# A two-layer decoder trunk: the norm's factor moved from y to the gate sums and the down outputs, y-combinations formed one stage earlier, two plain pairs per layer instead of six

## The chip, the core and the metric

One of the eight cores of a Trainium2 chip runs the whole program. The metric is device time in microseconds (us) of one execution, the lower the better.

## What is computed

The input is one sequence of 512 tokens with 1024 features, in float32. Layer 0 mixes tokens with an mLSTM and a differential attention, layer 1 with a sparse attention (compressed, selected and window branches). Behind each mixer stands a gated feed-forward block, and at the end a norm. The change touches the feed-forward block, the output projection ahead of it and the residual sums behind it:

```python
def rmsnorm(x, g):
    y = xf * lax.rsqrt(jnp.mean(xf * xf, axis=-1, keepdims=True) + RMS_EPS)
    return y * g
...
def swiglu_ffn(h, norm_g, w_gate, w_up, w_down):
    y = rmsnorm(h, norm_g)
    return (jax.nn.silu(y @ w_gate) * (y @ w_up)) @ w_down
...
    h = h + mixer(...) @ w_out
    h = h + swiglu_ffn(h, ...)
```

FFN_HIDDEN is 2816, so w_gate and w_up have 22 blocks of 128 columns each. The factor of the norm is one number per token; below it is called the norm's factor (rinv in the code). The gain g is one number per feature.

## The kernel before

**Layout.** Everything is kept feature-major: 128 partitions hold 128 features, and the free dimension is the 512 tokens (T), so a 1024-feature array is eight blocks of 128x512 (KT = 8). Each float32 operand of a product is split in two: a high part (a copy to the type fp32r, made by ScalarE) and a low part (the rest, made by VectorE), and a product is three matmuls: high by high, high by low, low by high. w_high and w_low are the split weights, y_high and y_low the split input.

**The stream of weights.** The weights come in units of 128 output columns (UNIT_LIST), through a ring of four raw buffers that SyncE fills and two pairs of split buffers. A plain unit is eight feature blocks by three matmuls, 24 matmuls of 128x512. All engines run their own hand-written list in order and wait for each other by semaphores.

**The stages around the change**, once per layer: WO (8 units, output projection; VectorE adds each unit's result to the residual hT, ScalarE makes y_high with the gain, VectorE y_low, ScalarE the square, GpSimd adds the squares up in sum_square), UP (gate and up products), DN (down projection, 16 half units, residual add in down_post). TensorE turns the sum of squares into columns (norm_columns, L993), GpSimd takes the power -1/2, VectorE spreads it (norm_diag) and TensorE lays the factor out over the partitions (norm_rows, L998) into bank aux 1; ScalarE copies it to rinv. norm_columns stands behind the first UP unit in TensorE's list and norm_rows behind the second.

**Plain pairs.** A pair is block t of w_gate and block t of w_up. The first PLAIN = 6 pairs of a layer are two plain units each. Their y has the gain and not the norm's factor; VectorE multiplies the factor in when it takes a result out of its bank (take, L2173), ScalarE applies silu, GpSimd multiplies gate and up (L3054), ScalarE and VectorE split the product into ffn_high and ffn_low.

**Fast pairs.** The other NFAST = 16 pairs use a product of 2x2 blocks with seven block products instead of eight. Weights are combined into the forms A11, A12, S2, S1, S3, S4, A22 and the input into B11, B21, T2, T1, T3, B22, T4; a block product is 4 by 3 matmuls of 128x256, 84 matmuls for a pair. fast_quad is TensorE's list: the seven products in this order, with waits for the forms (form_low) and, before S2, S3, S4 and A22, for ScalarE to have copied the bank's half (part_taken, fast_copy, L1887), because three products are added up in the same half bank and intermediate sums are taken on the way. Since the input forms are made from scaled y, VectorE first makes eight blocks y_scaled (L2497, with gain and factor), then the sums T1, T2, T3, T4 (y_sum, 128x1024 each) and the seven low parts, all during the plain pairs.

For each fast pair VectorE's list in fast_up is, for pair t in the middle of the stage: s24_low and s13_low of t (L2572, L2566), fast_take of t-1 (L2586), first_sums of t+1 (L2550), the two halves of fast_product of t-1 (L2594, L2596), a22_low of t (L2578), gate_form_low of t+1 (L2539), ffn_low of t-1 (L2481), second_sums of t+1 (L2559, L2561). ScalarE's: a22_high, fast_copy A11, fast_silu of t-1 (L1893), gate_form_high of t+1 (L1844), fast_copy S2, fast_ffn_high of t-1, fast_copy S1, fast_copy S3, s24_high and s13_high of t+1 (L1862, L1853). GpSimd adds one 128x256 pair of partial sums (up_late, L3059), released by fast_copy S3.

The lines that say how a fast pair's gate sum gets to silu, on VectorE and ScalarE, are

```python
dve.wait_ge(S("part_taken"), 4 * fast_quads(layer, t) + 2)
dve.tensor_tensor(a, ps(tile)[:, :], a, ALU.add).then_inc(bank_free(tile), 1)
...
wait_taken(act, (f"UP{layer}", 2 * t))
act.activation(a, a, ACT.Silu).then_inc(S("silu"), 1)
```

## Time and profile before

| | before |
|---|---|
| median of 3 runs | 1299.47 us (1298.99 to 1299.5) |
| profiled execution, its own time | 1298.77 us |
| its span | 1297.0 us |
| TensorE matmul busy, share | 1285.3 us, 99% |
| TensorE weight loads busy, share | 1084.0 us, 84% |
| VectorE | 868.4 us, 67% |
| ScalarE | 654.4 us, 50% |
| GpSimd | 203.9 us, 16% |
| granted TensorE clock | full in all 40 slices |
| HBM | 95 GB/s over the span |

The span runs from the first to the last instruction of the profiled execution, and the execution's own time stands 1.77 us above it. Matmuls are pipelined and overlap in the records, so that the start of one to the start of the next is the pace of TensorE, not the duration of one. Likewise a VectorE or ScalarE instruction that waits for nothing starts a little before the one ahead of it has ended. In the timeline's rows the text in brackets is the idle time ahead of the instruction and what ended it.

### The profile page before, as it was taken

What the parts mean: (1) busy time and instruction counts of PE and PEld (TensorE: products, weight loads), DVE (VectorE), ACT (ScalarE), POOL (GpSimd) and SP (SyncE); (2) the same over time, 40 slices, a digit from 0 to 9 for tenths busy, and PEclk for the clock granted to TensorE, in tenths of its full rate; (3) what the DMA queues carried; (4) which work ended last, traced back from release to release, by engine and by line L of the source; (5) the groups of instructions that cost most, each with busy time, mean ns of one, the idle gap of its engine ahead of it and who ended that gap; (6) DMA issues with size and microseconds to landing.
All of it is one profiled execution on the core that took longest, in us unless ns stands there. A gap on an engine that the chain in (4) does not pass through costs nothing.

```text
span 1297.0 us, 20009 instructions
## 1 busy us (share of the span) xinstructions
PE 1285.3 (99%) x7568; PEld 1084.0 (84%) x7568; DVE 868.4 (67%) x1522; ACT 654.4 (50%) x1214; POOL 203.9 (16%) x212
## 2 busy tenths in 40 slices
PE   9999999999999999999999999999999999999997
PEld 7777788888999998888788865568888999998887
DVE  5678886558888884232699778776477888872222
ACT  4445765434566563222275457785444565652222
POOL 2003571222100011000000002112213101110100
PEclk9999999999999999999999999999999999999999
DMA  8332222342433348332244310000432334455311
GB/s 257 82 82 62 56 65 72 90 147 82 113 98 99 104 120 255 94 89 81 82 123 130 95 33 17 2 2 25 140 112 81 98 99 117 112 138 165 106 44 66
DMA packets 207177, 124.40 MB, mean 96 GB/s; under 512 B 5841, under 2 KB 203729, under 8 KB 206321
## 3 DMA queue, kind: packets, MB, share of 16 engines
q1 hardware_dynamic: 205936, 113.03, 30.9%
q10 hardware_dynamic: 736, 9.84, 2.0%
q0 software_dynamic: 416, 0.35, 0.3%
q8 instruction: 56, 0.92, 0.3%
q14 instruction: 33, 0.26, 0.1%
HBM read 116.92 MB, written 6.29 MB: 95 GB/s over the span
## 4 chain that ended last, share of the span: by engine, by line
PE 88%; DVE 6%; issue 2%; ACT 2%; POOL 2%; DMA 0%; SPq 0%; POOLq 0%; DVEq 0%; ACTq 0%
PE acc L881 12%; PE acc L883 11%; PE acc L882 11%; PE acc L1201 8%; PE acc L1203 8%; PE acc L1204 8%; PE acc L1532 3%; PE acc L894 2%; PE acc L895 2%; PE acc L898 2%; PE aux L1519 2%; PE aux L1439 2%; POOL work L3054 2%; DVE w_low L730 1%; PE acc L935 1%
## 5 line engine op out<-in xcount | busy, mean ns | idle before, releaser
L730 DVE TENSOR_TENSOR w_low<-raw_units,w_high 128x1024 fp32r<-128x1024 f32 (+1 forms) x120 | 161.7, 1347 | 233.2 <-ACT w_high L711 233.1
L711 ACT ACTIVATE w_high<-raw_units 128x1024 fp32r<-128x1024 f32 (+2 forms) x121 | 136.7, 1129 | 221.3 <-PE acc L883 183.2
L881 PE MATMUL acc<-y_high,w_high 128*128 128x512 f32 (+1 forms) x360 | 144.8, 402 | 0.0
L881 PE MATMUL acc<-ffn_high,w_high 128*128 128x512 f32 (+1 forms) x374 | 141.0, 377 | 0.0
L882 PE MATMUL acc<-ffn_low,w_high 128*128 128x512 f32 (+1 forms) x374 | 140.8, 377 | 0.0
L883 PE MATMUL acc<-ffn_high,w_low 128*128 128x512 f32 (+1 forms) x374 | 140.8, 377 | 0.0
L883 PE MATMUL acc<-y_high,w_low 128*128 128x512 f32 (+1 forms) x360 | 140.7, 391 | 0.0
L882 PE MATMUL acc<-y_low,w_high 128*128 128x512 f32 (+1 forms) x360 | 140.3, 390 | 0.0
L1201 PE MATMUL acc<-high_T,s_s_forms 128*128 128x256 f32 x384 | 108.8, 283 | 2.0 <-DVE s_s_forms L2572 2.0
L1204 PE MATMUL acc<-high_T,s_s_forms 128*128 128x256 f32 x384 | 108.7, 283 | 0.0
L1203 PE MATMUL acc<-low_T,s_s_forms 128*128 128x256 f32 x384 | 108.7, 283 | 0.0
L1887 ACT ACTIVATE work<-acc 128x256 f32<-128x256 f32 x128 | 49.2, 384 | 66.6 <-PE acc L1204 64.1
L882 PEld LDWEIGHTS acc<-ffn_low,w_high 128*128 128x128 f32 x374 | 70.4, 188 | 12.9
L883 PEld LDWEIGHTS acc<-ffn_high,w_low 128*128 128x128 f32 x374 | 70.4, 188 | 12.8
L881 PEld LDWEIGHTS acc<-ffn_high,w_high 128*128 128x128 f32 x374 | 70.4, 188 | 12.7
L883 PEld LDWEIGHTS acc<-y_high,w_low 128*128 128x128 f32 (+1 forms) x360 | 67.0, 186 | 15.3
L3059 POOL TENSOR_TENSOR work<-work 128x256 f32<-128x256 f32 x32 | 34.7, 1085 | 284.9 <-ACT work L1887 284.9
L881 PEld LDWEIGHTS acc<-y_high,w_high 128*128 128x128 f32 (+1 forms) x360 | 67.2, 187 | 14.5 <-issue 0.8
L882 PEld LDWEIGHTS acc<-y_low,w_high 128*128 128x128 f32 (+1 forms) x360 | 67.2, 187 | 14.1 <-issue 0.5
L2099 ACT ACTIVATE score<-score,neg_max 128x384 f32<-128x384 f32 (+3 forms) x128 | 68.7, 541 | 18.7 <-DVE neg_max L2918 18.5
L3040 POOL TENSOR_TENSOR work<-work,work 128x512 f32<-128x512 f32 x31 | 42.1, 1357 | 225.2 <-ACT work L1625 224.8
L1201 PEld LDWEIGHTS acc<-high_T,s_s_forms 128*128 128x128 f32 x384 | 73.7, 192 | 2.3 <-DVE s_s_forms L2572 2.3
(410 smaller groups left out, 3313.7 us busy)
## 6 DMA issues: line engine op xcount, KB each, us to landing
raw_units<-in_l_w_gate_dram SPq DMA_DIRECT2D x44, 512.0 KB, 5.2
raw_units<-in_l_w_up_dram SPq DMA_DIRECT2D x44, 512.0 KB, 4.0
raw_units<-in_l_w_down_dram SPq DMA_DIRECT2D x32, 704.0 KB, 4.7
raw_units<-in_l_w_in_dram SPq DMA_DIRECT2D x43, 512.0 KB, 3.9
raw_units<-in_l_w_out_dram SPq DMA_DIRECT2D x16, 512.0 KB, 4.0
residual_spill<-residual ACTq DMA_DIRECT2D x2, 2048.0 KB, 7.4
residual<-residual_spill ACTq DMA_DIRECT2D x2, 2048.0 KB, 10.8
raw_units<-in_l_w_in_dram SPq DMA_DIRECT2D x10, 256.0 KB, 3.1
```

What stands on the lines that cost most here:

```text
L711: act.activation(dst, src, ACT.Copy).then_inc(S("split_high"), 1)
L730: dve.tensor_tensor(dst, src, high.bitcast(F32), ALU.subtract).then_inc(S("split_low"), 1)
L881: pe.matmul(o, ah, bh, start=first, stop=False)
L882: pe.matmul(o, ah, bl, start=False, stop=False)
L883: return pe.matmul(o, al, bh, start=False, stop=last)
L1201: pe.matmul(out, wh_k, y_high_of[y][:, c], start=start and k == 0, stop=False, skip_group_check=True)
L1203: pe.matmul(out, wh_k, y_low_of[y][:, c], start=False, stop=False, skip_group_check=True)
L1204: mm = pe.matmul(out, wl_k, y_high_of[y][:, c], start=False, stop=(k == KT // 2 - 1), skip_group_check=True)
L1532: mm = pe.matmul(ps(("OB", b))[64 * g:64 * g + 64, :].rearrange("p (h q) -> p h q", q=P), vsw[:, v:v + HD], probs[:, 4 * g:4 * g + 4, col(s)],
L1887: act.activation(dst, src, ACT.Copy).then_inc(S("part_taken"), 1)
L2099: act.activation(probs_at(n), probs_at(n), ACT.Exp, scale=-1.0, bias=nmx[:, n % 16:n % 16 + 1], accum_out=rsum[:, n % 16:n % 16 + 1]).then ...
L3040: pool.tensor_tensor(tmp[0][:, 0:T], tmp[0][:, 0:T], tmp[1 + m % 2][:, 0:T], ALU.add)\
```

## The change

The line numbers in the code shift by up to about 60. What it does:

- PLAIN goes from 6 to 2 in both layers, NFAST from 16 to 20; the plain path for a layer without fast pairs, which no layer used, goes away.
- The input forms are made from y with the gain and without the norm's factor. So y_scaled and its eight VectorE instructions go, and B11, B21 and B22 are no forms of their own any more: fast_quad reads quarters of y_high and y_low.
- ScalarE writes y a third time, as plain float32 (y_raw), in each WO unit. VectorE makes T1, T2, T3, T4 from it in the last four WO units (y_sums, four 128x256 instructions per unit, released by the square's semaphore sq). The high part of T2 stands on ScalarE ahead of the split of the third UP unit, T1's and T3's behind the split of the fourth; T4's goes where y's B12 quarter lies, behind the last plain unit.
- fast_take multiplies the gate sum by the factor in aux bank 1, with one more VectorE instruction that waits for the one ahead of it. The up sums stay without the factor.
- down_post multiplies the down projection's output by rinv before it is added to the residual, again one more instruction that waits for the one ahead; so do the two halves of the last tile. For it ScalarE copies the factor to rinv again at the end of UP.
- In plain pairs VectorE multiplies gate and up itself when it takes the up result (ffn_post), and GpSimd's product goes.
- Some semaphores are merged (s_recip into s_coef, rinv_count, parts_summed); loads, their sizes and their order on SyncE's queue follow the same table with more fast units.

```diff
-FAST = (0, 1)
-PLAIN = 6
+PLAIN = 2
...
-Y_FORMS = ("B11", "B21", "T1", "B22", "T2", "T3", "T4")
+Y_SUMS = ("T2", "T1", "T3", "T4")
...
@@ fast_quad, TensorE
-                    if t == PLAIN:
+                    if t == PLAIN and y in Y_SUMS:
                         pe.wait_ge(S("form_low"), y_split(layer, y))
...
@@ post of a WO unit, ScalarE
                     norm_y(n, j)
                     if j == 7:
                         split_high(act, u + SPL)
+                    act.activation(y_raw[:, tcol(j)], hT[:, tcol(j)], ACT.Copy, scale=par[:, gain_at(n, j)])
                     square(n, j)
...
@@ fast_up, ScalarE
-                hi_at = {3: ["B11"], 4: ["B21"], 5: ["T1"], 6: ["B22"], 7: ["T2"], 8: ["T3"], 9: ["T4"]}
+                hi_at = {1: ["T1", "T3"]}
                 act.dma_start(spill, hT).then_inc(S("residual_moved"), 16)
+                y_form_high(layer, "T2")
                 for c in range(2 * PLAIN):
...
                     ffn_post(layer, c // 2, c % 2)
+                y_form_high(layer, "T4")
                 for t in range(PLAIN, HT):
                     a22_high(layer, t)
                     fast_copy(layer, t, "A11")
...
                 fast_silu(layer, HT - 1)
+                act.activation(rinv, aux[:, 1, :], ACT.Copy).then_inc(S("rinv"), 1)
...
@@ post of a WO unit, VectorE
                     norm_low(1 + 2 * int(name[2]), j)
                     if j == 7:
                         split_low(dve, u + SPL)
+                    if j >= 4:
+                        y_sums(int(name[2]), j - 4)
...
+            def y_sums(layer, k):
...
+                dve.wait_ge(S("sq"), 16 * layer + k + 5)
+                dve.tensor_tensor(t1, b11, b12, ALU.subtract).then_inc(S("form_sums"), 1)
+                dve.wait_ge(S("form_sums"), base + 1)
+                dve.scalar_tensor_tensor(out=t2, in0=t1, scalar=-1.0, in1=b22, op0=ALU.mult, op1=ALU.subtract)\
+                   .then_inc(S("form_sums"), 1)
+                dve.tensor_tensor(b12, b22, b12, ALU.subtract).then_inc(S("form_sums"), 1)
+                dve.wait_ge(S("form_sums"), base + 2)
+                dve.scalar_tensor_tensor(out=t4, in0=t2, scalar=-1.0, in1=b21, op0=ALU.mult, op1=ALU.subtract)\
+                   .then_inc(S("form_sums"), 1)
...
@@ fast_take, VectorE
-                dve.tensor_tensor(a, ps(tile)[:, :], a, ALU.add).then_inc(bank_free(tile), 1)
+                dve.tensor_tensor(a, ps(tile)[:, :], a, ALU.add).then_inc(S("part_summed"), 1)
+                dve.wait_ge(S("part_summed"), parts_summed(layer, t))
+                dve.tensor_tensor(a, a, aux[:, 1, :], ALU.mult).then_inc(bank_free(tile), 1)
...
@@ down_post, VectorE
-                dve.tensor_tensor(hT[:, tile_at(m, it, 2)], ps(tile)[:, :], hT[:, tile_at(m, it, 2)], ALU.add)\
-                   .then_inc(bank_free(tile), 1)
+                h, part = hT[:, tile_at(m, it, 2)], tmp[3][:, 0:T]
+                dve.tensor_tensor(part, ps(tile)[:, :], rinv, ALU.mult).then_inc(S("part_summed"), 1)
+                dve.wait_ge(S("part_summed"), parts_summed(layer, HT - 1, m) + it * 2)
+                dve.tensor_tensor(h, part, h, ALU.add).then_inc(bank_free(tile), 1)
...
@@ fast_up, VectorE
-                scaled_at = {1: (0, 1, 2), 2: (3, 4, 5), 3: (6, 7)}
-                sum_at = {3: 1, 4: 2, 5: 3, 7: 4}
-                low_at = {4: ["B11"], 5: ["B21"], 6: ["T1", "B22"], 7: ["T2"], 8: ["T3"], 9: ["T4"]}
+                low_at = {1: ["T2", "T1", "T3"]}
...
                     if t > PLAIN:
                         fast_take(layer, t - 1)
                     else:
+                        y_form_low(layer, "T4")
                         ffn_low(layer, t - 1)
...
@@ ffn, GpSimd
-                def product(t, it=0):
...
-                    pool.tensor_tensor(up, tmp[2 * (t % 2)][:, 0:T], up, ALU.mult).then_inc(S("ffn_prod"), 1)
```

**VectorE, a fast pair in the middle of the stage.** work is the buffer of a gate or up sum, acc a PSUM bank, s_s_forms the forms S1 to S4, aux bank 1 the norm's factor. Before:

```order
L2572 TENSOR_TENSOR s_s_forms<-raw_units,s_s_forms 128x2x512
L2566 TENSOR_TENSOR s_s_forms<-s_s_sums_149,s_s_forms 128x2x512
L2586 TENSOR_TENSOR work_62<-acc,work_62 128x512
L2550 TENSOR_TENSOR s_s_sums_148<-raw_units 128x2x512
L2594 SCALAR_TENSOR_TENSOR work_63<-work_63,work_62 128x256
L2596 SCALAR_TENSOR_TENSOR work_63<-acc,work_62 128x256
L2578 TENSOR_TENSOR a_low<-raw_units,a_high 128x512
L2539 TENSOR_TENSOR gate_form_low<-raw_units,gate_form_high 128x1024
L2481 TENSOR_TENSOR ffn_low<-work_63,ffn_high 128x512
L2559 TENSOR_TENSOR raw_units<-s_s_sums_148,raw_units 128x512
L2561 TENSOR_TENSOR raw_units<-raw_units 128x512
```

and now:

```order
L2529 TENSOR_TENSOR s_s_forms<-raw_units,s_s_forms 128x2x512
L2523 TENSOR_TENSOR s_s_forms<-s_s_sums_140,s_s_forms 128x2x512
L2543 TENSOR_TENSOR work_60<-acc,work_60 128x512
L2545 TENSOR_TENSOR work_60<-work_60,aux 128x512
L2507 TENSOR_TENSOR s_s_sums_141<-raw_units 128x2x512
L2553 SCALAR_TENSOR_TENSOR work_61<-work_61,work_60 128x256
L2555 SCALAR_TENSOR_TENSOR work_61<-acc,work_60 128x256
L2535 TENSOR_TENSOR a_low<-raw_units,a_high 128x512
L2496 TENSOR_TENSOR gate_form_low<-raw_units,gate_form_high 128x1024
L2467 TENSOR_TENSOR ffn_low<-work_61,ffn_high 128x512
L2516 TENSOR_TENSOR raw_units<-s_s_sums_141,raw_units 128x512
L2518 TENSOR_TENSOR raw_units<-raw_units 128x512
```

Behind fast_take (the line with acc,work) stands the multiply by aux; all else is in the order it had.

**VectorE, the last two WO units.** y_raw is y with the gain, raw_T a raw T1, T2 or T4. Before:

```order
L2149 SCALAR_TENSOR_TENSOR y_low_164<-residual,feature_params,y_high_156 128x512
L2388 TENSOR_TENSOR residual<-acc,residual 128x512
L2149 SCALAR_TENSOR_TENSOR y_low_165<-residual,feature_params,y_high_157 128x512
L730 TENSOR_TENSOR w_low_57<-raw_units,w_high_56 128x1024
L730 TENSOR_TENSOR w_low_59<-raw_units,w_high_58 128x1024
L2162 TENSOR_SCALAR msq<-aux 128x4
```

and now:

```order
L2115 SCALAR_TENSOR_TENSOR y_low<-residual,feature_params,y_high 128x512
L2440 TENSOR_TENSOR raw_T_143<-y_raw 128x256
L2442 SCALAR_TENSOR_TENSOR raw_T_144<-raw_T_143,y_raw 128x256
L2444 TENSOR_TENSOR y_raw<-y_raw 128x256
L2446 SCALAR_TENSOR_TENSOR raw_T_145<-raw_T_144,y_raw 128x256
L2354 TENSOR_TENSOR residual<-acc,residual 128x512
L2115 SCALAR_TENSOR_TENSOR y_low<-residual,feature_params,y_high 128x512
L734 TENSOR_TENSOR w_low_57<-raw_units,w_high_56 128x1024
L2440 TENSOR_TENSOR raw_T_143<-y_raw 128x256
L2442 SCALAR_TENSOR_TENSOR raw_T_144<-raw_T_143,y_raw 128x256
L2444 TENSOR_TENSOR y_raw<-y_raw 128x256
L2446 SCALAR_TENSOR_TENSOR raw_T_145<-raw_T_144,y_raw 128x256
```

Four instructions (raw_T, raw_T, y_raw, raw_T) stand between a unit's y_low and the next unit's residual sum, and four behind the split of the second UP unit's weights, ahead of the split of the third's and of msq.

**ScalarE, the way into the first fast pair.** ffn_high is made from the product of the last plain pair, a_high is A22's high part, and the line work<-acc is the copy that TensorE's S2 waits for. Before:

```order
L1862 ACTIVATE s_s_forms<-raw_units 128x2x512
L1853 ACTIVATE s_s_forms<-s_s_sums_149 128x2x512
L1808 ACTIVATE ffn_high<-work_63 128x512
L1871 ACTIVATE a_high<-raw_units 128x512
L1887 ACTIVATE work_60<-acc 128x256
L1844 ACTIVATE gate_form_high<-raw_units 128x1024
```

and now:

```order
L1842 ACTIVATE s_s_forms<-raw_units 128x2x512
L1833 ACTIVATE s_s_forms<-s_s_sums_141 128x2x512
L1791 ACTIVATE ffn_high<-work_63 128x512
L1812 ACTIVATE y_high<-raw_T_145 128x4x256
L1851 ACTIVATE a_high<-raw_units 128x512
L1864 ACTIVATE work_60<-acc 128x256
L1824 ACTIVATE gate_form_high<-raw_units 128x1024
L1864 ACTIVATE work_60<-acc 128x256
```

The high part of T4 (y_high<-raw_T) stands between ffn_high and A22's; all else is in the order it had.

## Rows read from the trace of the kernel before

**Rows 1.** Windows view, fast pairs of layer 0: PE, PEld, DVE, ACT, POOL busy, clock, DMA.

```profile
334.40:497.00 162.60, 161.61 (x1346) 161.40 (x1346) 133.93 (x173) 98.76 (x160) 18.66 (x17) 1.00 0.40 107
```

**Rows 2.** Timeline, TensorE: last WO unit, first UP unit, norm_rows (start, us, instruction, [idle]).

```profile
261.87 0.39 PE L881 MATMUL acc<-mix_high_m,w_high 128*128 128x512 f32 x1
...
267.31 0.39 PE L881 MATMUL acc<-y_high,w_high 128*128 128x512 f32 x1
...
279.14 1.02 PE L998 MATMUL aux<-work,shape_constants 128*128 128x512 f32 x2
```

**Rows 3.** Timeline, VectorE, one fast pair in the middle of layer 0.

```profile
355.66 1.23 DVE L2572 TENSOR_TENSOR s_s_forms<-raw_units,s_s_forms 128x1024 fp32r<-128x1024 f32 x1 [1.65 <-ACT s_s_forms L1862]
...
357.94 0.68 DVE L2586 TENSOR_TENSOR work<-acc,work 128x512 f32<-128x512 f32 x1
...
359.67 0.42 DVE L2594 SCALAR_TENSOR_TENSOR work<-work,work 128x256 f32<-128x256 f32 x1
...
362.08 0.68 DVE L2481 TENSOR_TENSOR ffn_low<-work,ffn_high 128x512 fp32r<-128x512 f32 x1
362.68 0.69 DVE L2559 TENSOR_TENSOR raw_units<-s_s_sums,raw_units 128x512 f32<-128x512 f32 x1
363.40 0.69 DVE L2561 TENSOR_TENSOR raw_units<-raw_units 128x512 f32<-128x512 f32 x1
```

**Rows 4.** Timeline, ScalarE, the same pair.

```profile
357.45 0.38 ACT L1887 ACTIVATE work<-acc 128x256 f32<-128x256 f32 x1 [0.35 <-PE acc L1204]
358.66 0.63 ACT L1893 ACTIVATE work<-work 128x512 f32<-128x512 f32 x1 [0.82 <-DVE work L2586]
359.20 1.04 ACT L1844 ACTIVATE gate_form_high<-raw_units 128x1024 fp32r<-128x1024 f32 x1
360.33 0.39 ACT L1887 ACTIVATE work<-acc 128x256 f32<-128x256 f32 x1
...
364.65 1.06 ACT L1862 ACTIVATE s_s_forms<-raw_units 128x1024 fp32r<-128x1024 f32 x1 [1.06 <-PE acc L1204]
```

**Rows 5.** Timeline, GpSimd's partial sum, of the pair of rows 3 and twelve pairs later.

```profile
363.67 1.02 POOL L3059 TENSOR_TENSOR work<-work 128x256 f32<-128x256 f32 x1 [9.06 <-ACT work L1887]
...
484.63 1.02 POOL L3059 TENSOR_TENSOR work<-work 128x256 f32<-128x256 f32 x1 [9.07 <-ACT work L1887]
```

**Rows 6.** Timeline, GpSimd, the last plain product of layer 0.

```profile
335.62 1.30 POOL L3054 TENSOR_TENSOR work<-work,work 128x512 f32<-128x512 f32 x1 [6.34 <-DVE work L2173]
```

**Rows 7.** Timeline, VectorE, at the same time as rows 6.

```profile
335.92 2.08 DVE L2572 TENSOR_TENSOR s_s_forms<-raw_units,s_s_forms 128x1024 fp32r<-128x1024 f32 x1 [0.45 <-ACT s_s_forms L1862]
```

**Rows 8.** Timeline, VectorE, WO units 6 and 7 of layer 0.

```profile
264.37 0.68 DVE L2388 TENSOR_TENSOR residual<-acc,residual 128x512 f32<-128x512 f32 x1
...
267.51 0.69 DVE L2388 TENSOR_TENSOR residual<-acc,residual 128x512 f32<-128x512 f32 x1 [0.92 <-PE acc L883]
...
269.94 1.23 DVE L730 TENSOR_TENSOR w_low<-raw_units,w_high 128x1024 fp32r<-128x1024 f32 x1 [0.20 <-ACT w_high L711]
```

**Rows 9.** Timeline, ScalarE, WO unit 6 of layer 0: y_high and the square.

```profile
265.08 0.72 ACT L1618 ACTIVATE y_high<-residual,feature_params 128x512 fp32r<-128x512 f32 x1 [1.89 <-DVE residual L2388]
265.72 0.62 ACT L1625 ACTIVATE work<-residual 128x512 f32<-128x512 f32 x1
```

**Rows 10.** Timeline, GpSimd, the last sum of squares of WO in layer 0.

```profile
270.51 1.81 POOL L3040 TENSOR_TENSOR work<-work,work 128x512 f32<-128x512 f32 x1 [2.76 <-ACT work L1625]
```

**Rows 11.** Timeline, TensorE, behind the first UP unit of layer 0: norm_columns.

```profile
272.75 0.95 PE L993 MATMUL aux<-shape_constants,work 128*128 128x2 f32 x8
```

**Rows 12.** Timeline, VectorE, split of the fourth UP unit of layer 0.

```profile
283.73 1.23 DVE L730 TENSOR_TENSOR w_low<-raw_units,w_high 128x1024 fp32r<-128x1024 f32 x1 [2.20 <-ACT w_high L711]
```

**Rows 13.** Timeline, TensorE, the first S2 of layer 0.

```profile
338.47 0.35 PE L1201 MATMUL acc<-high_T,s_s_forms 128*128 128x256 f32 x1 [0.99 <-DVE s_s_forms L2572]
```

**Rows 14.** Timeline, GpSimd, the last sum of squares of DN in layer 0.

```profile
621.26 1.29 POOL L3040 TENSOR_TENSOR work<-work,work 128x512 f32<-128x512 f32 x1 [12.96 <-ACT work L1625]
```

**Rows 15.** Timeline, TensorE, the norm_columns that waits for rows 14.

```profile
622.60 0.83 PE L993 MATMUL aux<-shape_constants,work 128*128 128x2 f32 x6 [0.21 <-POOL work L3040]
```

331 lines of the change are left out of this document (119 added, 212 removed).

## The prediction

> **What bounds the kernel now.** I read the page's busy times first, then the stretches of the feed-forward block, then the timelines of each engine there. In the fast pairs of layer 0 TensorE's matmuls and its weight loads are both busy for 161 of 162.6 us, VectorE for 134, ScalarE for 99, at full clock [rows 1]. So TensorE sets the pace, and the first term of any change is what its list gains. A WO or UP unit is 5.44 us from start to start (261.87 to 267.31) [rows 2], a plain pair 10.88. GpSimd's partial sum comes once per fast pair, 12 pairs in 120.96 us, so a fast pair is 10.08 us and one of its seven products 1.44 [rows 5].
>
> The question is how much room the others have, and a busy share doesn't tell. In one fast pair VectorE starts s24_low at 355.66 and ends second_sums at 364.09 (363.40 + 0.69): 8.43 us without a gap. It then idles 1.65 us for ScalarE's high part of S2 and S4 (L1862) [rows 3]. That instruction was released at 364.65 by TensorE and takes 1.06 [rows 4]. Had TensorE been earlier, it could have started at 364.13. So VectorE's own round is 8.43 + 0.04 + 1.06 + 0.04 = 9.57 us, **0.5 us under TensorE's 10.08**. 1.1 of the 1.65 idle us are a wait that no faster TensorE removes.
>
> **The change part by part.** All sums are against the profiled execution, 1298.77 us, which lies 0.7 under the median; I add 0.7 at the end.
>
> *Four more fast pairs per layer.* 4 x (10.88 - 10.08) = 3.2 us off TensorE's list per layer, if the pairs keep 10.08.
>
> *The multiply in fast_take.* It reads 512 elements and waits for the instruction ahead, as L2561 waits for L2559: 0.72 us from start to start (362.68 to 363.40) [rows 3]. VectorE's round becomes 8.43 + 0.73 + 1.14 = 10.29 us, 0.21 over TensorE's pace. There is a second effect. Silu (358.66) waits for fast_take, gate_form_high (359.20) for silu, and the copy of S2's sum (360.33) stands behind both; TensorE's S3 waits for that copy [rows 4]. The quad starts 1.55 us ahead of the copy A11 at 357.45, at 355.90, so S3 is due at 355.90 + 4 x 1.44 = 361.66. With the multiply the copy starts at 360.88 and S3 may start about 0.5 later, 361.36: 0.3 us are left. They are used up in one or two pairs, and then TensorE waits ahead of every S3.
>
> GpSimd adds to it. Its 128x256 sum takes 1.02 us from 363.67 and ends at 364.69, 0.60 behind the end of VectorE's L2561 [rows 3, 5]: it waited for VectorE and works about 0.65. The other way round, VectorE's L2572 took 2.08 instead of 1.23 while GpSimd's sum ran until 336.92 [rows 6, 7]. So two such instructions with all operands in SBUF exclude each other. Before the change GpSimd was asked at the end of VectorE's run and worked in its idle time. Now the run is 0.73 longer and the request falls ahead of or into L2559. Behind L2559 VectorE waits for its own result, GpSimd gets in, and L2561 starts about 0.33 late (0.65 less what overlaps); if GpSimd gets in one instruction earlier it is 0.46. Round: 10.62, bounds 10.29 (never gets in) and 10.75. I take 10.62, because a waiting engine meets a gap there. 18 rounds lie between the second and the last fast pair: 18 x (10.62 - 10.08) - 0.3 = **+9.4 us per layer**, bounds +3.4 and +11.7.
>
> The page SBUF — State Buffer of the Trainium skill (section Who interferes with whom) says that whoever issues first holds the shared port pair for the whole instruction and the other fully blocks. By that alone GpSimd would pay and not VectorE in half of the cases, and the sum would lie between my two bounds; the rows agree with the rule and do not tell who wins at a gap.
>
> *y_raw and the y sums in WO.* ScalarE's y_raw costs what y_high does, 0.64 (265.08 to 265.72) [rows 9], ahead of the square. The four sums are 128x256, 0.34 to 0.42 each [rows 3], the second waiting for the first: 1.5 us, if GpSimd stays out. But sq releases them and GpSimd's sum of squares together. GpSimd (1.29 when alone [rows 14], 1.81 behind VectorE's split [rows 8, 10]) gets in at the wait, and VectorE is done 2.5 us behind the square. From a unit's residual sum to there it is now 0.71 + 0.64 + 0.63 + 0.62 + 2.5 = 5.1 us; with the next split's 1.14 that is 6.2, more than a unit's 5.44. So the residual sums of units 5, 6 and 7 slip, 0.8, 1.6 and then 3.5 us: the last one from 267.51 to 271.06 [rows 8]. TensorE first waits for the last y_low in the first UP unit (due 272.07, there 273.3), then norm_columns, until now at 272.75 [rows 11], waits for the last sum of squares, which ends at about 276.2 instead of 272.32. **+3.5 us per layer**. Lower bound 1.1 (the sums fit between the units, only y_raw and the last sums count), upper 4. I take 3.5, since both engines were seen waiting for each other [rows 6, 7, 10].
>
> *The way into the first fast pair.* In the clock of the old trace and without the delay above, norm_rows stands at 279.14 [rows 2] and two more units end at 290.9. VectorE splits the fourth unit at 283.73 [rows 12]. Behind that stand the product (0.60), three low forms T2, T1, T3 (1.14 each), first_sums (1.14) and gate_form_low (1.23), which ends at 291.3: A11 waits 0.4. Then two second sums and a take end at 293.4, and ScalarE does silu, S24, S13, ffn_high, T4 (0.95), A22 and the copy A11: S2 can start at 298.3, against 294.2 by TensorE. Before, S2 waited 1.15, 0.99 of it in the record [rows 13]. So 0.4 + 4.1 - 1.15 = **+3.4 us per layer**. Six plain pairs had hidden these forms; two do not. Bounds 1 (the queues overlap better than I add them up) and 4.
>
> *Removed:* eight y_scaled, three low forms, GpSimd's plain products. They lay beside plain units without a gap on TensorE: worth nothing, and their room goes with the four pairs. Reading y_high in strides of quarters: nothing, since the block read has 256 elements either way. Loads: the 16 DMA engines are busy 40% in the fast pairs [rows 1]; nothing.
>
> *down_post.* One more dependent instruction per tile, 0.73. Seven tiles hide it behind 14.96 us of matmuls. The last tile of layer 0 does not: its residual goes through square and GpSimd's sum (621.26) to a norm_columns that already waits 0.21 (622.60) [rows 14, 15]: **+0.7**. The last tile of layer 1 ends the program; its half is 256 wide, 0.42 + 0.04 [rows 3]: **+0.5**. Nothing from other edits: the renamed semaphores change no order, and rinv's second copy (0.5) lies 7 us ahead of its use.
>
> **Sum.** Per layer -3.2 + 9.4 + 3.5 + 3.4 = 13.1; twice 26.2; with 0.7 and 0.5, 27.4. 1298.77 + 27.4 = 1326.2, and 1326.9 as a median; I say 1326.5. With the upper bounds of the round and of WO it is 2 x 2.8 more, 1333.
>
> **The rivals.**
> - *GpSimd never costs VectorE anything.* The round is 10.29 and WO loses 2.2. Per layer -3.2 + 3.4 + 2.2 + 3.4 = 5.8; 1298.77 + 11.6 + 1.2 + 0.7 = 1312. For it: so far GpSimd was the one that waited [rows 5, 10]. Against: VectorE waited too [rows 6, 7]. Chance 0.27.
> - *The fast pairs stay at 10.08.* The page Perfetto Trace Analysis of the Trainium skill (Identifying the Most-Contended Engine) would rank TensorE by the busy share of its weight loads and optimize the most contended engine first; by this rule VectorE's 0.73 is hidden. The weight loads are busy 161.4 of 162.6 us [rows 1], which speaks for it. Then only the stage's start costs: -3.2 + 3.5 + 3.4 per layer, 1308. Decides: the multiply costs VectorE under 0.5 us. The 0.72 from L2559 to L2561 speaks against [rows 3]. Chance 0.08.
> - *Faster: the sums and forms are hidden and the pairs keep 10.08.* One mechanism: VectorE's queue never becomes the last wait in WO and UP, because ScalarE and TensorE run ahead of it by more than I read. Then -6.4 + 1.2: 1294. It decides when VectorE is free within 5.44 us in WO and within 10.08 in UP; I find 6.2 and 10.3 to 10.6. Chance 0.07.
> - *The terms cancel* by half costs at the starts and 10.08: 1299. Chance 0.03.
> - My forecast, 1324 to 1333 by its bounds: 0.55.
>
> **How the numbers follow.** 0.2% of this time, 2.6 us, is what a measurement can tell from no change. Slower holds forecast and the first two rivals, 0.90; faster 0.07; the same 0.03. The range goes from the second rival, 1307, to the forecast's upper bound, 1333; outside lie the last two rivals and a bit at the ends.
>
> **What would show it.** In the profile after: GpSimd's partial sums in UP 10.3 to 10.8 us apart instead of 10.08, from the third fast pair on; TensorE idle ahead of each S3 (released by the copy of S2's sum), some 0.2 to 0.6 us; VectorE idle only 1.1 us per pair; L2561's successor or GpSimd's sum lengthened. norm_columns (L993's successor) waiting 2 to 4 us for GpSimd in both layers; the first S2 waiting about 4 us; VectorE's last residual sum of WO 1 to 3.5 us behind TensorE. I am wrong if the partial sums stay 10.08 us apart, or if the norm_columns behind the first UP unit doesn't wait.

## The result, and the profile after

The kernel before took 1299.26 us (median of 4 runs, 1298.99 to 1299.5), the changed one **1343.72 us** (4 runs, 1342.76 to 1345.34): the ratio is **1.0336, 95% interval 1.0323 to 1.035**. The direction was forecast, the size was not: 1326.5 with a range of 1307 to 1333.

Three lines of the page of the changed kernel: busy time of the engines, the clock granted to TensorE in 40 slices, and the chain that ended last.

```profile
PE 1302.1 (97%) x7856; PEld 1104.3 (82%) x7856; DVE 942.5 (70%) x1629; ACT 672.0 (50%) x1274; POOL 191.6 (14%) x208
...
PEclk9999999988999999999999999999989999999999
...
PE 58%; DVE 27%; ACT 9%; issue 4%; POOL 1%; DMA 0%; DVEq 0%; ACTq 0%; SPq 0%; POOLq 0%
```

The chain of the kernel before:

```profile
PE 88%; DVE 6%; issue 2%; ACT 2%; POOL 2%; DMA 0%; SPq 0%; POOLq 0%; DVEq 0%; ACTq 0%
```

VectorE's share of the chain was 6% before, it is 27% now. TensorE's busy share does not show this: it is still 97%, with TensorE's share of the chain down from 88% to 58%. And the clock line has dips, at the starts of both feed-forward blocks.

The waits of TensorE (source, us in total, times, longest), the changed kernel:

```profile
PE acc L1190 <- ACT work L1864: 14.3, 34, 0.5
PE acc L1190 <- DVE s_s_forms L2523: 7.7, 2, 3.9
PE aux L982 <- POOL work L2981: 4.0, 3, 1.9
PE acc L870 <- DVE y_low L2115: 3.9, 3, 2.1
```

These are the four places that the forecast named: S3 in nearly every fast pair, the first S2 of each layer, norm_columns, and the last low part of y. To see where the 45 us went I cut both executions at the same landmarks: ScalarE's copy of the norm's factor from `aux` (start of L1612, before L1629), and GpSimd's first and last partial sum of a layer (L2994, before L3059). Before is corrected by the four plain pairs that became fast ones (4 x 10.88 taken from the stretch ahead of the first partial sum, 4 x 10.08 added to the partial sums).

| stretch | before | after | longer | forecast |
|---|---|---|---|---|
| start to the copy, layer 0 | 280.20 | 288.47 | 8.3 | 3.5 |
| copy to the first partial sum | 63.31 - 43.52 = 19.79 | 25.58 | 5.8 | 3.4 |
| first to last partial sum | 151.30 + 40.32 = 191.62 | 203.65 | 12.0 | 9.4 |
| last one to the copy in layer 1's attention | 135.32 | 137.17 | 1.9 | 0.7 |
| from there to the copy in its feed-forward block | 317.43 | 323.87 | 6.4 | 3.5 |
| copy to the first partial sum | 63.32 - 43.52 = 19.80 | 25.26 | 5.5 | 3.4 |
| first to last partial sum | 191.62 | 203.52 | 11.9 | 9.4 |
| last one to the end | 134.82 | 134.78 | 0.0 | 0.5 |
| fast for plain, 8 pairs | | | -6.4 | -6.4 |
| sum | 1297.0 | 1342.3 | 45.3 | 27.4 |

One correction to read it rightly: the last partial sum is not the end of UP. TensorE's last matmul of UP starts 2.00 us behind it in the kernel before, but 1.49 and 1.47 us behind it in the changed one, where ScalarE's split of the next weights, ahead of the copy that releases the sum, ends later. So 0.5 us of each 12.0 and 11.9 belongs to the row below it: the pairs cost 11.5 and 11.4 us, and the ends 2.4 and 0.5.

**The fast pairs.** Windows view of 15 periods of GpSimd's partial sum (columns as in [rows 1]): the period is 161.55 / 15 = 10.77 us. TensorE, busy 161.61 of 162.60 before, has 6.5 us of idle time now.

```profile
345.46:507.01 161.55, 155.01 (x1262) 151.96 (x1262) 142.71 (x182) 88.43 (x150) 18.25 (x15) 1.00 0.36 99
```

The timeline of VectorE in one pair, of ScalarE in the same, of GpSimd at two sums, and of TensorE around S3:

```profile
391.50 1.23 DVE L2529 TENSOR_TENSOR s_s_forms<-raw_units,s_s_forms 128x1024 fp32r<-128x1024 f32 x1 [1.19 <-ACT s_s_forms L1842]
...
393.78 0.68 DVE L2543 TENSOR_TENSOR work<-acc,work 128x512 f32<-128x512 f32 x1
394.50 0.69 DVE L2545 TENSOR_TENSOR work<-work,aux 128x512 f32<-128x512 f32 x1
...
398.65 0.68 DVE L2467 TENSOR_TENSOR ffn_low<-work,ffn_high 128x512 fp32r<-128x512 f32 x1
399.25 0.69 DVE L2516 TENSOR_TENSOR raw_units<-s_s_sums,raw_units 128x512 f32<-128x512 f32 x1
399.97 1.11 DVE L2518 TENSOR_TENSOR raw_units<-raw_units 128x512 f32<-128x512 f32 x1
```

```profile
395.22 0.63 ACT L1870 ACTIVATE work<-work 128x512 f32<-128x512 f32 x1 [2.01 <-DVE work L2545]
...
396.71 0.36 ACT L1864 ACTIVATE work<-acc 128x256 f32<-128x256 f32 x1
```

```profile
388.56 1.21 POOL L2994 TENSOR_TENSOR work<-work 128x256 f32<-128x256 f32 x1 [9.55 <-ACT work L1864]
399.32 1.21 POOL L2994 TENSOR_TENSOR work<-work 128x256 f32<-128x256 f32 x1 [9.55 <-ACT work L1864]
```

```profile
396.42 0.28 PE L1193 MATMUL acc<-high_T,s_s_forms 128*128 128x256 f32 x1
397.12 0.39 PE L1190 MATMUL acc<-high_T,s_s_forms 128*128 128x256 f32 x1 [0.42 <-ACT work L1864]
397.35 0.28 PE L1192 MATMUL acc<-low_T,s_s_forms 128*128 128x256 f32 x1
```

The multiply (L2545) starts 0.72 us behind the sum, as rows 3 had priced it. GpSimd's sum is on record from 399.32, while L2516 still runs, until 400.53. VectorE's last sum (L2518), 0.69 us before, starts at 399.97 and takes 1.11: GpSimd got in at the dependent gap behind L2516, and VectorE pays 0.42. VectorE idles 1.19 per pair instead of 1.65 [rows 3]: from the end of L2518 at 401.08 to 402.27, all of it ScalarE's high part of S2 and S4 (1.06 us, released by L2518), the part that no faster TensorE removes. On TensorE the whole loss sits at S3: 0.70 and 0.23 from start to start where two matmuls of a quad take 0.24 together, 0.69 per pair.

**The start of a block, and the clock.** TensorE in layer 0: the wait for the last y_low, norm_columns, two of the slow matmuls behind it; then the first S2.

```profile
274.87 0.50 PE L870 MATMUL acc<-y_high,w_high 128*128 128x512 f32 x1 [2.15 <-DVE y_low L2115]
...
277.75 1.62 PE L982 MATMUL aux<-shape_constants,work 128*128 128x2 f32 x8 [1.91 <-POOL work L2981]
...
279.80 0.63 PE L871 MATMUL acc<-y_low,w_high 128*128 128x512 f32 x1
280.23 0.63 PE L872 MATMUL acc<-y_high,w_low 128*128 128x512 f32 x1
...
306.53 0.55 PE L1190 MATMUL acc<-high_T,s_s_forms 128*128 128x256 f32 x1 [3.85 <-DVE s_s_forms L2523]
```

The same two places as windows:

```profile
279.23:284.49 5.26, 5.26 (x13) 4.11 (x14) 1.99 (x3) 1.45 (x2) 1.03 (x1) 0.50 0.60 173
306.53:312.00 5.47, 5.47 (x26) 5.47 (x26) 5.23 (x7) 1.23 (x2) 0.00 (x0) 0.50 0.27 77
```

The granted clock is 0.50 in both, the lower of the two levels (1.2 GHz instead of 2.4), and a matmul takes twice its time from start to start: 0.43 instead of 0.227 us at 512 columns, 0.21 instead of 0.12 at 256. In both places TensorE had just idled: 2.15 and 1.91 us with three matmuls between, and 3.85 us. In the kernel before it had idled about a microsecond at the first S2 [rows 13] and its mean clock was 0.999; now it is 0.988. About 2.7 us are lost behind norm_columns and 2.4 behind the first S2 in layer 0; in layer 1 it is 2.1 (970.13 to 974.47) and 2.2 (996.80 to 1001.63). A fifth low stretch stands at the end of layer 0, where TensorE had waited only 0.58 and 0.20 us:

```profile
644.57:654.87 10.30, 10.10 (x38) 7.73 (x39) 1.99 (x3) 1.06 (x1) 2.13 (x2) 0.83 0.21 59
```

No step of the prediction held this.

VectorE and GpSimd at WO units 6 and 7 of layer 0, with the y sums behind unit 6 between them:

```profile
267.54 0.68 DVE L2354 TENSOR_TENSOR residual<-acc,residual 128x512 f32<-128x512 f32 x1
...
270.15 0.42 DVE L2440 TENSOR_TENSOR raw_T<-y_raw 128x256 f32<-128x256 f32 x1 [0.38 <-ACT work L1608]
270.61 1.40 DVE L2442 SCALAR_TENSOR_TENSOR raw_T<-raw_T,y_raw 128x256 f32<-128x256 f32 x1
...
272.60 0.68 DVE L2354 TENSOR_TENSOR residual<-acc,residual 128x512 f32<-128x512 f32 x1
```

```profile
270.19 1.53 POOL L2981 TENSOR_TENSOR work<-work,work 128x512 f32<-128x512 f32 x1 [4.66 <-ACT work L1608]
276.19 1.50 POOL L2981 TENSOR_TENSOR work<-work,work 128x512 f32<-128x512 f32 x1 [4.47 <-ACT work L1608]
```

The four sums take 2.5 us (270.15 to 272.67), as forecast, since GpSimd's sum of squares gets in at the second. The residual sum of unit 7 stands at 272.60, where the forecast had 271.06 and rows 8 had 267.51; the last sum of squares at 276.19 ends at 277.7 instead of 276.2.

### The profile page after: what moved, and what is told of

Same layout as the page of the kernel before. It is cut to its first block, busy times and chain, and to the rows that moved or that the text cites. A ratio compares the mean times of both kernels' runs of the same rounds, so it can differ in the third digit from the quotient of the medians.

```text
span 1342.3 us, 20796 instructions
## 1 busy us (share of the span) xinstructions
PE 1302.1 (97%) x7856; PEld 1104.3 (82%) x7856; DVE 942.5 (70%) x1629; ACT 672.0 (50%) x1274; POOL 191.6 (14%) x208
## 4 chain that ended last, share of the span: by engine, by line
PE 58%; DVE 27%; ACT 9%; issue 4%; POOL 1%; DMA 0%; DVEq 0%; ACTq 0%; SPq 0%; POOLq 0%
PE acc L870 9%; PE acc L872 9%; PE acc L871 9%; DVE s_s_forms L2523 3%; DVE gate_form_low L2496 3%; ACT s_s_forms L1842 3%; DVE raw_units L2518 3%; DVE s_s_forms L2529 3%; PE acc L1515 3%; PE acc L883 2%; PE acc L884 2%; PE acc L887 2%; PE aux L1502 2%; DVE work L2545 2%; DVE raw_units L2516 2%
## 5 line engine op out<-in xcount | busy, mean ns | idle before, releaser
L1190 PE MATMUL acc<-high_T,s_s_forms 128*128 128x256 f32 x480 | 141.8, 295 | 22.0 <-ACT work L1864 14.3
L1193 PE MATMUL acc<-high_T,s_s_forms 128*128 128x256 f32 x480 | 137.6, 287 | 0.0
L1190 PEld LDWEIGHTS acc<-high_T,s_s_forms 128*128 128x128 f32 x480 | 94.0, 196 | 29.2 <-ACT work L1864 21.2
L2994 POOL TENSOR_TENSOR work<-work 128x256 f32<-128x256 f32 x40 | 48.5, 1213 | 423.6 <-ACT work L1864 423.6
L870 PE MATMUL acc<-y_high,w_high 128*128 128x512 f32 (+1 forms) x232 | 97.3, 419 | 3.9 <-DVE y_low L2115 3.9
L1192 PEld LDWEIGHTS acc<-low_T,s_s_forms 128*128 128x128 f32 x480 | 94.3, 196 | 0.0
L1193 PEld LDWEIGHTS acc<-high_T,s_s_forms 128*128 128x128 f32 x480 | 94.0, 196 | 0.0
L872 PE MATMUL acc<-y_high,w_low 128*128 128x512 f32 (+1 forms) x232 | 92.5, 399 | 0.0
L871 PE MATMUL acc<-y_low,w_high 128*128 128x512 f32 (+1 forms) x232 | 92.2, 397 | 0.0
L1190 PE MATMUL acc<-y_high,gate_form_high 128*128 128x256 f32 x320 | 90.8, 284 | 0.4 <-DVE gate_form_low L2496 0.4
L1192 PE MATMUL acc<-y_low,gate_form_high 128*128 128x256 f32 x320 | 90.6, 283 | 0.0
L1193 PE MATMUL acc<-y_high,gate_form_low 128*128 128x256 f32 x320 | 90.5, 283 | 0.0
L2529 DVE TENSOR_TENSOR s_s_forms<-raw_units,s_s_forms 128x1024 fp32r<-128x1024 f32 x40 | 49.0, 1226 | 51.2 <-ACT s_s_forms L1842 51.2
```

The costliest lines, as they stand in the source:

```text
L870: pe.matmul(o, ah, bh, start=first, stop=False)
L871: pe.matmul(o, ah, bl, start=False, stop=False)
L872: return pe.matmul(o, al, bh, start=False, stop=last)
L1190: pe.matmul(out, wh_k, y_high_of[y][yk], start=start and k == 0, stop=False, skip_group_check=True)
L1192: pe.matmul(out, wh_k, y_low_of[y][yk], start=False, stop=False, skip_group_check=True)
L1193: mm = pe.matmul(out, wl_k, y_high_of[y][yk], start=False, stop=(k == KT // 2 - 1), skip_group_check=True)
```

## The experiments

Theory A: each fast pair lasts as long as VectorE's round, and the round grew by the multiply and by GpSimd's intrusion. Theory B: TensorE's waits at the start of a block cost twice, once as idle time and once as a lower clock behind them. The rivals stand in the expectations. Ratios are against the kernel before, whose median was 1299.0 to 1299.5 us beside each of them. Of an edit its main lines are shown; where an instruction moves or goes, the semaphore counts that others wait for follow.

### The multiply taken out

```
-                dve.tensor_tensor(a, ps(tile)[:, :], a, ALU.add).then_inc(S("part_summed"), 1)
-                dve.wait_ge(S("part_summed"), parts_summed(layer, t))
-                dve.tensor_tensor(a, a, aux[:, 1, :], ALU.mult).then_inc(bank_free(tile), 1)
+                dve.tensor_tensor(a, ps(tile)[:, :], a, ALU.add).then_inc(bank_free(tile), 1)
```

> The changed kernel without the multiply by the norm's factor in fast_take; the gate's sums stay without the factor. Theory A (VectorE's round sets the fast pair: 9.57 us of its own work as before, 0.73 for the multiply, 0.46 for GpSimd's sum that gets in ahead of the last sum): the pairs go back to 10.08 us, which takes 12.0 and 11.9 us off the two layers, 1343.7 - 23.9 = 1320. Rival (the pairs are slow for another reason, such as the y blocks read in strides of quarters or the clock): pairs stay at 10.76 us, 1343 to 1344.

1318.87 us (ratio 1.0151, 1.0134 to 1.0168). The partial sums are 10.08 us apart in both layers, as Theory A said (1320), and the stride of the y blocks and the number of fast pairs cost the pairs nothing. The gate's sums of this kernel lack the factor.

### The multiply alone, in the kernel before

The sum and the multiply of the changed kernel, put into fast_take of the kernel before (with two semaphores of layer 1's attention merged into one, as in the change; its stretch there stays as long as it was, 317.4 us). The gate's sums then hold the factor twice.

> The kernel before with the dependent multiply alone in fast_take (the gate's sums then hold the factor twice). Theory A: the multiply alone makes the fast pairs 10.76 us; 16 pairs per layer, the first two still at TensorE's pace, about 13.5 x 0.68 = 9.2 us per layer, 1299.3 + 18.4 = 1317.7. Rival (the stride of the y blocks or the later start of the quads is needed as well): pairs at 10.1 to 10.3, under 1306.

1316.48 us (1.0132, 1.0115 to 1.0149). Periods 10.08, 10.55 and then 10.76; L2561 takes 1.11 us at the median, where it took 0.69. That is the changed kernel's period, so one added instruction of 0.69 us explains the whole loss of the pairs, GpSimd's part included.

### GpSimd's partial sum made narrow

```
-                    pool.tensor_tensor(b[:, 256:512], b[:, 0:256], b[:, 256:512], ALU.add).then_inc(S("up_late"), 1)
+                    pool.tensor_tensor(b[:, 256:258], b[:, 0:2], b[:, 256:258], ALU.add).then_inc(S("up_late"), 1)
```

> The changed kernel with GpSimd's partial sum over 2 of its 256 columns; the rest of that half of up lacks one part. Theory A: without GpSimd on VectorE's way the round is 9.57 + 0.73 = 10.30 us, 17 to 18 pairs per layer x 0.46 = 8 us, 1343.7 - 16 = 1328. Rival (the chain from the take over silu, gate_form_high and the copy of S2's sum to S3 sets the pair, not VectorE's own list): pairs stay over 10.6 us and under 5 us are gained, 1339 to 1344.

1329.9 us (1.0234, 1.0217 to 1.0251), pairs 10.34 us apart, as Theory A said; the kernel leaves out most of a partial sum. VectorE's last sum in this kernel (duration min/median/max in ns):

```profile
L2518 DVE TENSOR_TENSOR raw_units<-raw_units x40: 691/692/694, 301.1 to 1184.2; 128x512 f32<-128x512 f32 x40
```

in the changed kernel:

```profile
L2518 DVE TENSOR_TENSOR raw_units<-raw_units x40: 691/1111/1116, 300.3 to 1197.5; 128x512 f32<-128x512 f32 x40
```

So of the 0.68 us per pair 0.42 are GpSimd's and 0.26 the multiply's, the rest of which fits under TensorE's 10.08.

### TensorE kept busy in its waits

```
+            def repeat(count, cols=T):
+                for _ in range(count):
+                    pe.matmul(aux[:, 0, 0:cols], yh[:, 0:P], yh[:, 0:cols], start=True, stop=True)
```

Nine of 512 columns ahead of the wait for the last y_low, eight ahead of norm_columns, 30 of 256 ahead of the first S2.

> The changed kernel with matmuls whose result nobody reads in TensorE's three long waits per layer (9 and 8 of 512 columns around norm_columns, 30 of 256 ahead of the first S2). Theory (the waits let the granted clock fall to the 1.2 GHz level for 13 matmuls of 512 columns and 26 of 256, which cost 2.6 and 2.4 us per layer on the critical path): the clock stays at full speed and 10.0 us go, 1343.7 - 10 = 1334, up to 1 us less gained where a repeat is in the way. Rival 1 (the clock falls there for another reason, such as the 334 GB/s of loads and the spill in the same stretch): nothing gained, 1344 to 1346. Rival 2 (VectorE's queue sets the stage's start, so a faster TensorE only waits longer): clock full, but under 4 us gained, 1340 or more.

1332.41 us (1.0256, 1.0239 to 1.0273), mean clock 0.998. Two stretches of it, around norm_columns and the first S2:

```profile
274.00:286.00 12.00, 11.82 (x53) 8.92 (x52) 6.37 (x9) 4.81 (x7) 2.56 (x2) 1.00 0.79 262
300.00:309.00 9.00, 8.75 (x73) 8.57 (x72) 8.62 (x10) 5.68 (x10) 0.28 (x1) 1.00 0.13 37
```

The waits were as long as before and only filled, and 11.3 us went. 262 GB/s of loads ran beside the first stretch at full clock, so the loads are not the reason (rival 1), and the lost time was on the path (rival 2 falls). By stretches of the two profiled executions, 3.2 and 2.6 us went around norm_columns and 2.5 and 2.1 between there and the first partial sum. The other 1.7 us went at the end of layer 0, where no wait was filled: the waits there are 0.58 and 0.21 us in this run too, and the clock simply did not fall. So about 10 of the 11.3 us are what the filled waits gave back. This kernel is also the changed one without the clock's share, and can be cut at the same landmarks, each stretch from the copy before it: WO 4.8 and 3.8 us longer than before, the way to the first partial sum 3.3 and 3.3, the partial sums 12.0 and 11.8, layer 0's end 0.2, layer 1's end 0.0 (with the 0.5 us of the last partial sum's place: pairs 11.4 and 11.3, ends 0.7 and 0.5).

### The y sums a unit later

```
-                    if j >= 4:
-                        y_sums(int(name[2]), j - 4)
+                    for k in {5: (0,), 6: (1,), 7: (2, 3)}.get(j, ()):
+                        y_sums(int(name[2]), k)
```

> The changed kernel with the y sums of each of the last four WO units behind the next unit's residual sum and low part (the last two groups both behind unit 7's). Theory (the sums of VectorE wait for ScalarE's square and push the residual sums back, and so delay the first UP unit and norm_columns by 4.8 us): the residual sums follow TensorE within 2 us again, the wait for the last y_low (2.15 us) goes and norm_columns waits 1.5 to 2.5 us; 2.5 to 3 us per layer, 1338; if the clock then holds, 2.6 more per layer, 1333. Rival (y_raw on ScalarE and GpSimd's sum set the time, not VectorE's sums): under 1 us per layer, 1342 to 1344.

1337.67 us (1.0296, 1.0277 to 1.0314): 3.0 us per layer. The wait for the last y_low falls from 2.15 to 0.24 us, norm_columns still waits:

```profile
272.95 0.50 PE L870 MATMUL acc<-y_high,w_high 128*128 128x512 f32 x1 [0.24 <-DVE y_low L2115]
275.82 1.05 PE L982 MATMUL aux<-shape_constants,work 128*128 128x2 f32 x8 [1.91 <-POOL work L2981]
```

norm_columns stands 1.9 us earlier than in the changed kernel. The clock still fell behind it, for 7 matmuls of 512 columns instead of 12. The residual sums were read too simply in the expectation: unit 7's is at 270.67, 3.2 us behind the kernel before. The starts show why. Before, those of units 1 to 3 follow each other at 239.40, 243.79 and 248.17, 4.39 us apart: VectorE's queue comes out of the attention late and catches up with units of 5.44. In the changed kernel they are at 240.29, 245.25 and 250.20, 4.95 us apart: y_raw, on ScalarE between y_high and the square, slows the catching up by 0.56 us per unit, ahead of any y sum.

### All y sums in UP

The sums moved behind norm_diag, T2's high part behind the copy of the factor.

> The changed kernel with all sixteen y sums moved from WO to UP, behind norm_diag, and T2's high part behind the copy of the factor. WO: norm_columns only 0.6 to 1 us later than in the kernel before, no fall of the clock there: 4.1 + 2.6 = 6.7 us gained per layer. UP: 6 us more in VectorE's queue ahead of the first fast pair; theory (VectorE's queue sets the start of the fast pairs): the first S2 waits 3 to 6 us longer, in all 1336 to 1342. Rival (ScalarE's queue sets that start): the 6 us lie beside it, 1330 to 1332.

1334.7 us (1.0267, 1.0249 to 1.0285). WO loses 0.2 us against the kernel before (from the first copy of a factor in the program to this one: 252.3 against 252.1), though y_raw is still in it: VectorE has caught up by unit 7. So y_raw alone costs next to nothing there, and it is the y sums behind it that find no room. The start of the fast pairs pays instead: a unit waits 2.73 us for its low weights and the first S2 3.25 us (2.72 and 2.99 in layer 1), all released by VectorE, and the clock falls behind each of them. VectorE's queue sets that start, as the theory had it, but the 6 us of sums cost less there than it said: the time is 9.0 us under the changed kernel's, between the theory's 1336 and the rival's 1332.

### T4 behind A22 and A11's copy

```
-                y_form_high(layer, "T4")
                 for t in range(PLAIN, HT):
                     a22_high(layer, t)
                     fast_copy(layer, t, "A11")
+                    if t == PLAIN:
+                        y_form_high(layer, "T4")
```

(and its low part behind a22_low)

> The changed kernel with T4's high and low parts behind a22_high and the copy of A11's sum instead of ahead. Theory (ScalarE's 0.95 us for T4 stand on the way to the copy that S2 waits for): S2's wait falls from 3.85 to 2.9 us, 1.8 us in all, 1342; the clock falls all the same. If 2.9 us of waiting no longer let the clock fall, 4.8 more, 1337. Rival (S2 waits for VectorE's low parts, released by the last plain product): nothing, 1343.7.

1338.83 us (1.0307, 1.0286 to 1.0328), 4.9 us less than the changed kernel. But the four executions fall into two groups: 1336.91 and 1337.05 us at a mean clock of 0.993 and 0.994, and 1340.61 and 1341.31 at 0.988. The profile is of the one with 1337.05. The first S2 of its layer 0:

```profile
305.48 0.35 PE L1190 MATMUL acc<-high_T,s_s_forms 128*128 128x256 f32 x1 [2.91 <-issue]
```

The wait is 0.94 us shorter, as the theory said, and in this execution the clock did not fall behind 2.91 us of idle time (2.89 in layer 1): the first matmul takes 0.35 us instead of 0.55. The two executions that took about 4 us longer have the mean clock of the changed kernel, which fits a fall behind this wait; their traces are not kept, so that is likely and not shown. Of the 6.7 us that the shorter wait and the full clock should have given, 1.2 went to the fast pairs: T4's low part now stands in the first one, which is 10.54 us instead of 10.08, and first to last partial sum is 0.6 us longer per layer. The end of layer 0, which keeps its full clock here, gave 1.6 more, so that this execution is 7.0 us under the changed kernel's profiled one.

### Six plain pairs

`PLAIN = 6` in the changed kernel.

> The changed kernel with six plain pairs per layer as before, the rest of the change kept. Four pairs go from 10.76 to 10.88 us, +1.0 in all. Theory (two plain pairs are too few to hide the forms; with six the first S2 waits about 1.15 us as before and the clock holds there): 3.4 + 2.4 us less per layer, 1343.7 + 1.0 - 11.6 = 1333. Rival (the forms' order on ScalarE and VectorE sets the wait whatever the number of plain pairs): 1344 to 1345.

1334.65 us (1.0264, 1.0245 to 1.0282). Eight more plain pairs, at 10.88 against 10.76, and it is 9.1 us faster: no fall of the clock at the first S2, whose wait is 1.5 us, as the theory said (1333). At the changed kernel's own pace the exchange of plain for fast pairs was worth 1.0 us and cost 10.

### ffn_low in VectorE's idle time

```
-                    if t > PLAIN:
-                        ffn_low(layer, t - 1)
                     if t + 1 < HT:
                         second_sums(layer, t + 1)
+                    if t > PLAIN:
+                        ffn_low(layer, t - 1)
+                    if t + 1 < HT:
                         s24_low(layer, t + 1)
```

> The changed kernel, nothing left out, with ffn_low of the pair before moved behind second_sums in VectorE's order, into the 1.1 us in which VectorE waits for ScalarE's high part of S2 and S4. Theory A (VectorE's round of 10.76 us sets the fast pair): the round becomes 10.76 - 1.10 = 9.7 us, under TensorE's 10.08, and the pairs are 10.08 us apart: 1343.7 - 23.9 = 1320. Rival (what binds is the chain fast_take, silu, gate_form_high, copy of S2's sum, S3, and it is as long as before): pairs stay over 10.3 us, 1328 or more.

1330.94 us (1.0244, 1.0227 to 1.0261), pairs 10.35 us: the numbers of the rival (over 10.3 us, 1328 or more) and not Theory A's 10.08. That does not make its mechanism right: with GpSimd's sum moved besides (the run with both edits below) the pairs pass at 10.08, and the chain that the rival names is untouched by that. I had the whole 1.10 us of idle time in mind, but ffn_low is 0.60 us from start to start (398.65 to 399.25 above), and without it between them the first of second_sums waits for gate_form_low (1.32 us from start to start instead of 1.14). 0.42 came back.

### GpSimd's sum in VectorE's idle time

```
                     pool.wait_ge(S("part_taken"), 4 * fast_quads(layer, t) + 4)
+                    if t + 1 < HT:
+                        pool.wait_ge(S("form_sums"), forms_summed(layer, t + 1) + 3)
```

alone:

> The changed kernel, nothing left out, with GpSimd's partial sum released by second_sums of the next pair instead of by the copy of S3's sum alone, so that it falls into VectorE's idle 1.1 us. Theory A: the last sum takes 0.69 us again instead of 1.12, the round is 10.76 - 0.43 = 10.33 us: 19 periods x 0.43 less the first two, 7.3 us per layer, 1343.7 - 15 = 1329, as with the narrow partial sum (1329.9). Rival (GpSimd then pushes s24_low back by as much): nothing, 1343.

and with the edit before:

> e10's order (ffn_low, 0.60 us long, behind second_sums, pairs 10.35 us) and GpSimd's partial sum behind second_sums. If the two terms add, VectorE's round is 10.35 - 0.43 + 0.1 = 10.0 us, TensorE sets the pace again at 10.08: 1343.7 - 23.9 = 1320. Rival (GpSimd waits for ffn_low and then pushes s24_low back by 0.3): pairs at 10.2 to 10.3 us, 1325 to 1329.

Alone 1330.66 us (1.0239, 1.0223 to 1.0254), periods 10.34, L2518 at 0.69 us at the median. Together **1318.01 us** (1.0144, 1.0128 to 1.0159), periods 10.08. Both came close to what was expected (1329 and 1320). The two terms add, and a later start of GpSimd's sum, a wait more, takes 13 us off the program. The missing 0.27 us of the experiment before were GpSimd's.

### Mended schemes, and the kernel before with five plain pairs

The mended scheme has the edits on ffn_low and T4, y_raw behind the square (released by the next unit's square or the factor's copy), the y sums in UP's first two units, and T2, T1 and T3 spread over the third and fourth (with four plain pairs: third to fifth).

> The changed scheme mended: e10's order; y_raw behind the square; the y sums in UP's first two units; T4 behind a22_high and A11's copy; four plain pairs. Against the kernel before: 4 more fast pairs in all at 10.08 instead of 10.88, -3.2; WO +0.3 per layer; the first S2 waits about 1 us as before or up to 1 us more; layer 0's end +0.7: 1299.3 - 3.2 + 0.6 + 0.7 = 1297.4, up to 1301 where the start waits. If the fast pairs are not back at 10.08: 1315 or more.

> The same with three plain pairs: -4.8 from the pairs, +0.6 WO, +0.7 layer 0's end, and one unit pair less to hide the forms: VectorE's queue ahead of the fast pairs is 2 to 3 us too long, so the first S2 waits 1 to 3 us more per layer: 1297.8 to 1302; with a wait of 3.8 us the clock falls and it is 2.4 more per layer.

1306.83 us (1.0058, 1.0044 to 1.0072) and 1306.28 us (1.0056, 1.0042 to 1.0069). Both missed their expectations (1297.4 to 1301, 1297.8 to 1302). The starts are mended (clock 0.999 and 0.998, first S2 waiting 0.6 us), but the pairs are at 10.35, and 17 or 18 periods of 0.27 us in two layers are 9.2 and 9.7 us.

> The kernel before with five plain pairs per layer instead of six, the y forms finished two units earlier (normed y, no multiply). Two more fast pairs in all: -1.6 us, 1297.7, if VectorE's three low forms in one unit are hidden; with 1 to 2 us more waiting ahead of the first fast pair 1299 to 1301.

1308.17 us (1.0062, 1.0049 to 1.0076), 7 us over the top of the expectation. The pairs keep 10.08, but the first partial sum comes 5.9 and 5.1 us later than five plain pairs would give: A11 waits up to 2.7 us for gate_form_low, S2 up to 3.1, and the mean clock is 0.995. In the kernel before, too, the sixth plain pair hides the y forms, at least in this order of them; no other was tried.

With GpSimd's sum moved as well, three and two plain pairs:

> The mended scheme with three plain pairs (1306.3 us, pairs 10.35 us) and GpSimd's partial sum behind second_sums. If the pairs come back to 10.08, 18 periods x 0.27 per layer = 9.7 us less in all: 1296.6, faster than the kernel before (1299.2) by 0.2%. Rival as for e11: 1302 to 1305.

> The same with two plain pairs: 1.6 us less for the pairs against three, 1295.0, if the forms stay hidden; but VectorE's queue is then 3 us per layer too long ahead of the fast pairs (the first S2 waited 3.85 us in the changed kernel): +5 to +10, 1300 to 1306.

Three plain pairs: **1296.73 us** (11 runs, 1296.47 to 1298.78), ratio **0.9986, 0.9977 to 0.9995**, as expected (1296.6). So it is faster than the changed kernel by 47 us and than the one before by 0.14%, which is small, with the interval ending at 0.05%; but all eleven executions lie below all fifteen of the kernel before beside them (1298.8 to 1299.6). Two plain pairs: 1306.28 us (1.0057, 1.0043 to 1.0071), at the top of the expectation: A11 waits 3.74 us for gate_form_low and runs at the lower clock behind it. The chain of the kernel with three:

```profile
PE 93%; ACT 2%; DVE 1%; issue 1%; POOL 1%; DMA 0%; SPq 0%; POOLq 0%; DVEq 0%; ACTq 0%
```

and VectorE and GpSimd in a pair of it, where GpSimd's sum now ends in the gap behind ffn_low:

```profile
392.71 0.69 DVE L2517 TENSOR_TENSOR raw_units<-raw_units 128x512 f32<-128x512 f32 x1
393.32 0.68 DVE L2466 TENSOR_TENSOR ffn_low<-work,ffn_high 128x512 fp32r<-128x512 f32 x1
394.74 1.23 DVE L2528 TENSOR_TENSOR s_s_forms<-raw_units,s_s_forms 128x1024 fp32r<-128x1024 f32 x1 [0.73 <-ACT s_s_forms L1842]
```

```profile
393.55 1.06 POOL L3002 TENSOR_TENSOR work<-work 128x256 f32<-128x256 f32 x1 [9.02 <-DVE raw_units L2517]
```

## Why the prediction was right in direction and short by 17 us

The miss is 1343.7 - 1326.5 = 17.2 us. It splits into 11.3 us of clock (TensorE kept busy, with layer 0's end), 2.1 + 2.0 us of the pairs (11.5 and 11.4 against 9.4), 1.3 + 0.3 of WO (4.8 and 3.8 against 3.5), and 0.2 of the rest.

- *The missing step.* The prediction priced each wait of TensorE by its length and took "full clock" from [rows 1] for the whole program. It never asked what the clock does behind a longer wait, and so put this term at nothing without a reason. The kept-busy run shows the price, 11.3 us, against 27 us that were forecast in all: about 10 behind the long waits at the starts of the blocks, and 1.7 at the end of layer 0. What would have led there is that the trace of before has no wait of over 1.0 us in these blocks; a forecast of waits of 2 to 4 us left the ground on which its durations were read. The page TensorE: Matmul & The Clock Gate of the Trainium skill (Part 1: The HAM clock gate) says that "the default state is throttled, and activity releases the throttle", and gives 426.7 ns from start to start at 512 columns for the low state. The trace agrees: 0.43 us (279.80 to 280.23). The prediction did not use it.
- *The multiply in fast_take*: right. 0.72 us on VectorE's list, a round over TensorE's 10.08, TensorE waiting ahead of every S3 for the copy of S2's sum (0.42 us of waiting, forecast 0.2 to 0.6), VectorE idle about 1.1. The rival by which the pairs stay at 10.08 falls. With it falls, for these pairs, the ranking by busy share of the Trainium skill (Perfetto Trace Analysis, Identifying the Most-Contended Engine): TensorE's weight loads are busy 151.96 of 161.55 us and yet it is VectorE, busy 142.71 of them or 88%, that sets the pace.
- *GpSimd's exclusion*: right mechanism, mis-sized term. "L2561 starts about 0.33 late": it cost 0.42 us, as a longer L2518. The trace agrees with the rule of exclusion that the prediction named from the Trainium skill (SBUF — State Buffer, Who interferes with whom): GpSimd's sum is on record from 399.32 to 400.53, and L2518, started at 399.97, ended at 401.08. The round is 10.76, 0.14 over my 10.62 and a hair over the upper bound of 10.75: 0.09 for GpSimd (0.42 for 0.33) and 0.05 for VectorE's idle time (1.19 for 1.14). 17 periods of 0.14 are 2.4 us per layer; the first and the last pair cost less than a whole round, which leaves the 2.1 and 2.0. The first rival (GpSimd never costs VectorE) would be the narrow partial sum's 10.34, and that took removing it. With GpSimd's wait moved, though, the rival became true in the full kernel.
- *y_raw and the y sums in WO*: right mechanism, 3.5 forecast, 4.8 and 3.8 measured without the clock. The 2.5 us of the four sums were right. The step that failed is "the residual sums of units 5, 6 and 7 slip, 0.8, 1.6 and then 3.5 us": they slipped 2.4 (258.92 to 261.35), 3.2 and 5.1, and unit 4's by 1.7 already (0.2 of each is the later start of this execution). I had let VectorE start on time, while it was behind from the attention and catching up; y_raw slows that in every unit, so that the y sums met a queue that was already late. Without the y sums there it is caught up by unit 7.
- *The way into the first fast pair*: 3.4 forecast, 3.3 without the clock. The shape was as forecast, too: first S2 waiting 3.85 us behind T4 and the copy of A11.
- *Ends*: right. 0.7 and 0.5 were forecast. The table has 0.2 and 0.0 without the clock, and with the 0.5 us that the last partial sum stands later it is 0.7 and 0.5. The run without the multiply, where that sum stands as in the kernel before, shows it directly: 136.04 us against 135.32 at the end of layer 0 and 135.36 against 134.82 at the end of the program. In the changed kernel 1.7 us more go at layer 0's end, by the dip of the clock (0.83 from 644.57 to 654.87) that the kept-busy run doesn't have though its waits there are the same, 0.58 and 0.21 us. Why the clock dips there in some runs and not in others stays open.
- *Removed work and loads*: nothing, as forecast; the run without the multiply has its pairs at 10.08.
- *A sum that does not come out.* The prediction starts the copy of S2's sum at 360.88 with the multiply; by its own rows, 0.72 behind the silu at 358.66, gate_form_high and the copy follow at about 361.05, and S3 has 0.1 us of room instead of 0.3. It changes only the term of -0.3.

The range was too narrow mainly because both its ends came from mechanisms that the rows of before show, while the largest error began outside them. Without the clock the time was 1332.4, just inside the range.

## What to carry to other kernels

Compare the bound engine not with busy shares but with each other engine's round: its own work, plus the waits that no faster bound engine removes. Here 0.5 us of slack stood under 0.73 us of new work. When a change makes TensorE wait longer than it does anywhere in the trace at hand, price the matmuls behind the wait at the lower clock as well, as a cost that may come in one execution and not in the next, and consider filling the wait. And before moving work to save an engine time, look at who else is released there: one wait added to GpSimd's sum gave back 13 us.

## What was not expected of the hardware

- Idle TensorE can cost twice. Behind waits of 3.85 us (changed kernel), 3.74 (two plain pairs, mended), 3.25 and 2.73 (y sums in UP) matmuls ran at the 1.2 GHz level, and so they did behind 2.15 and 1.91 us with three matmuls between (1.20 and 1.91 in layer 1). Behind 2.91 us at the first S2 (T4 behind) the clock stayed full in both layers of the profiled execution, while two others of the same kernel took 4 us longer at a lower mean clock. At layer 0's end it fell behind 0.58 and 0.20 us in some runs and not in others. So the length of one wait does not decide alone, and what does is not shown here. With the long waits filled by matmuls that nobody reads, it did not fall anywhere.
- An SBUF-to-SBUF sum of GpSimd (128x256) that is asked for while VectorE works on SBUF operands costs VectorE 0.42 us per pair; released by VectorE's last sum, in VectorE's idle time, it costs VectorE nothing (L2518 is back at 0.69 us), and its own record is 0.74 us instead of 1.21.
